# The first decode batch's keys move into the last half pair of the prompt attention, and the attention's second group takes key blocks by two

## The chip, the cores and the metric

The kernel runs on one core of a Trainium2 chip. The metric is the device time of one execution in microseconds, from the start to the end of the program. Five engines run side by side, each through its own list of instructions in order: TensorE (matrix products and turns of blocks), VectorE, ScalarE, GpSimd, and SyncE, which issues transfers. They wait for each other on semaphores.

## What is computed

One inference step of a small hybrid decoder with two layers: a gated short convolution, then attention with forget gates over shared keys and values. It takes a prompt of 1024 tokens and, beside it, eight decode batches of eight tokens each, with 1024 past positions in pages of 128 that a table names. Cut to the two attentions:

```python
def prompt_attention(q, k, v, logf):          # 16 heads of 64, causal, by blocks of 128 queries
    s = einsum('bqhd,bkhd->bhqk', qb, k) * scale + c[t] - c[s]
    p = softmax(where(kpos <= qpos, s, NEG_INF))
    return einsum('bhqk,bkhd->bqhd', p, v)

def sample_attention(q, k_new, v_new, logf_new, k_past, v_past, logf_past):
    s_past = einsum('bqhd,bkhd->bhqk', q, k_past) * scale + cn_q + rest
    s_new  = einsum('bqhd,bkhd->bhqk', q, k_new) * scale + cn_q - cn
    p = softmax(concatenate([s_past, where(causal, s_new, NEG_INF)]))
    return einsum(p_past, v_past) + einsum(p_new, v_new)

x = x + (o * silu(z)) @ w_out                 # then a gated input embedding and a norm
```

## The kernel before

All orders are written by hand, for each engine, with semaphores between them. Products of the layers are made in three passes of split operands (a high and a low part: `w_hi`, `w_lo`, `Hhi`, `Hlo`).

**Prompt attention.** Heads go in eight pairs, `j` = 0 to 7; a pair is two half pairs, one for each head. `STEPS` is the order of a half pair. `("S", qb)` makes the scores of query block `qb` (VectorE takes the row maximum, L1647, ScalarE the exponential, L1249, GpSimd the normalisation, L579). `("T", grp, kb)` turns the probabilities of key block `kb` for the four query blocks of a group (L891); ScalarE copies them to `pTh` (L1257), VectorE subtracts for `pTl` (L1658). `("V", grp, kb)` multiplies them with the values (L903). `("D", n)` puts in `n` of the 48 dense pieces that make the next pair's projections, three passes each (L844 to L846). Two PSUM banks and two buffers serve the turned blocks, by `kb % 2`. In the second group a piece stands before each value product, and the turn of block `kb + 2` after it.

The last pair has no next pair to project for: its first half has 24 pieces, ahead of its second group, its second half has none. The half pairs of the last pair are called (7,0) and (7,1) here.

**Decode batches.** After the prompt attention, `sample_batch(b)` follows the list `BATCH`. `("K", pg)` turns a page of keys in two halves of four blocks (`k_turn`, L952), into PSUM banks 5 and 6; ScalarE copies the first half to `KT` (L1359), VectorE the second (L1770). `("B",)` starts the scores with the bias rows `Bkeys` (L961) and adds the new keys' scores (L964), `("S", pp)` adds the scores of two pages (L973). `Y`, `T` and `V` are the softmax's turns and the values of the batch before, `("D", n)` the dense pieces of the output projection (`out_pieces`, L1021 to L1023), 16 for each batch. The first batch has no batch before it: it runs with `first=True`, keys and scores alone.

Before the output projection can start, the eight blocks of the prompt's y have to be split into `Hhi` (ScalarE, `y_hi`, L1362) and `Hlo` (VectorE, `y_lo`, L1774); seven of them come back from memory. Before the first batch VectorE clears and fills the fixed rows of `Bkeys` (L1847 to L1852, semaphore `s_ones`) and arranges the queries (`prepare`); GpSimd then loads the bias rows (`load_sample`, L611 to L613).

Of the kernel before, what the change touches and what calls it, by code (L numbers as in the profile page):

```python
# [24 lines left out]
P = 128  # L25
D = 1024
# [38 lines left out]
         ("S", 6), ("D", 6), ("V", 0, 1), ("T", 0, 3), ("S", 7), ("D", 6), ("V", 0, 2), ("D", 1), ("V", 0, 3), ("D", 5),  # L65
         ("T", 1, 0), ("T", 1, 1)]
for _kb in range(8):
    STEPS += [("D", 1 if _kb < 7 else 2), ("V", 1, _kb)] + ([("T", 1, _kb + 2)] if _kb < 6 else [])
# [12 lines left out]
         ("K", 6), ("V", 5), ("V", 6), ("K", 7), ("V", 7), ("D", 4), ("S", 3)]  # L81
LAST = [("D", 3), ("Y",), ("T", 0), ("T", 1), ("T", 2), ("D", 2), ("V", 0), ("V", 1), ("V", 2), ("V", 3), ("D", 4),
# [20 lines left out]
def program(nc, a, o, d):  # L103

    es = ExitStack()
    with es:
# [37 lines left out]

        sh = ExitStack()
# [80 lines left out]
        SS = flat[:, 2 * 512:2 * 512 + NK]  # L226
        dcn = nc.dram_tensor("new_key_sums", (DB, 2, H, DS), F32, kind="Internal").ap()
# [21 lines left out]
        names += [f"k_in{i}" for i in range(RING)] + [f"v_in{i}" for i in range(RING)]  # L249
# [44 lines left out]
        def _(sp):  # L294
# [121 lines left out]
            def half1(j, more):  # L416
# [53 lines left out]
            for pg in range(RING):  # L470
                load_keys(0, pg, first=True)
            sp.wait_ge(sems["pv"], START["pv"] + 24 * NPAIR)
            load_x(0, 0)
            sample_loads(0, 0, x=False, tile=False)
# [41 lines left out]
        def _(g):  # L516
# [68 lines left out]

            def iteration(j, more):
                for hh in range(2):
                    if more and hh == 0:
                        gain_b1(j, 0, 1)
# [17 lines left out]
            def load_sample(b):  # L607

                rows = bass.ds(H * b, H)
                for x in range(2):  # L610
                    g.dma_start(f(Bk[H * x:H * x + H, 0:KEYS]), d["rest"][rows, x, 0:KEYS]).then_inc(sems["s_bk"], 16)  # L611
                    g.dma_start(f(Bk[H * x:H * x + H, KEYS:]), d["rest"][rows, x, bass.ds(KEYS + DS * b, DS)]).then_inc(sems["s_bk"], 16)
                g.dma_start(f(Ar[R_CN:R_CN + 2, :]), dcn[bass.ds(b, 1)].rearrange("b x h t -> (b x) (h t)")).then_inc(sems["s_bk"], 16)  # L613

# [29 lines left out]
            g.wait_ge(sems["s_restout"], 48)  # L644
            g.wait_ge(sems["s_ones"], 1)
            g.wait_ge(sems["kv_out"], START["kv_out"] + 64 * NPAIR)
# [6 lines left out]
            g.wait_ge(sems["s_all"], 1)  # L653
            load_sample(1)
# [13 lines left out]
        def _(pe):  # L668
# [237 lines left out]

            def half_pair(j, half, more):
                p = 0
                for step in STEPS:
# [34 lines left out]
            def k_turn(b, pg):  # L944

                pe.wait_ge(sems[f"k_in{pg % RING}"], 16 * (PAGES // RING * b + pg // RING) + 16)
                for c in range(2):
                    pe.wait_ge(sems[f"s_kt{c}"], START[f"s_kt{c}"] + PAGES * b + pg)
                    if pg == 2 and not (isinstance(b, int) and b == 0):
# [61 lines left out]
            def out_pieces(m, par, q0, n):  # L1011

                for q in range(q0, q0 + n):
                    blk, k = divmod(q, KC)
                    if q == 0:
# [12 lines left out]
            def sample_batch(b, par, first=False):  # L1028

                q = 0  # L1030
                for step in BATCH:
# [6 lines left out]
                    if step[0] == "Y" and not first and not (isinstance(b, int) and b == 1):  # L1038
                        s_y_turn(b - 2)
                    if step[0] == "T" and not first:  # L1040
                        s_p_turn(b - 1, step[1], PAGES * b + 2)
                    if step[0] == "V" and not first:
                        s_values(b - 1, step[1])
                    if step[0] == "D" and not first:
                        q = out_pieces(b - 1, 1 - par, q, step[1])

            pe.wait_ge(sems["s_ones"], 1)
# [48 lines left out]
        def _(act):  # L1096
# [208 lines left out]
            def beside(j, half, p, attend, more):  # L1305
# [58 lines left out]
            def probabilities(b):  # L1364

                act.wait_ge(sems["s_max"], b + 1)
                af(Ps[:, :], SS, ACT.Exp, bias=small[:, 0:1], accum_out=small[:, 1:2])
# [10 lines left out]
            def sample_batch(b, par, i):  # L1378
# [3 lines left out]
                keep_keys(b, 1)  # L1382
                turned_probabilities(b - 1)
                keep_keys(b, 2)
                keep_keys(b, 3)
                w_hi((N_B2 + par) % 2, B_B2 + 2 * b - 2, loaded(N_B2 + par, 2, i))
                for pg in range(4, PAGES):
                    keep_keys(b, pg)

            act.wait_ge(sems["o_done"], START["o_done"] + 4 * NPAIR)  # L1390
            y_hi(NPAIR - 1, yT[:, 0:SEQ])
            w_hi(N_B2 % 2, B_B2 - 3, loaded(N_B2))
            for pg in range(PAGES):
                keep_keys(0, pg)
# [527 lines left out]
```

## Time and profile before

| what | us |
|---|---|
| median of three runs | 1876.99 (1875.25 to 1880.03) |
| the profiled execution | 1878.54 |
| its span, first to last instruction | 1876.8 |
| TensorE busy in it | 1729.0 (92%) |
| VectorE, ScalarE, GpSimd busy | 861.3, 672.8, 324.1 |

The span is what the trace covers; the profiled execution's time holds a little more around it. Busy time of TensorE counts matrix products whose ends are modelled. The granted clock is told as a share of TensorE's full speed, so 1.00 is 2.4 GHz and 0.50 is 1.2 GHz. A time in brackets behind an instruction is the idle time of its engine before it, with what ended it.

### The profile page before, as it was taken

The page shows a single profiled execution, that of the slowest core. Times are in us where ns is not written, and L with a number is a line of the kernel's source. Part 1 is how long each engine was busy: PE and PEld are TensorE (multiplying, and loading weights), DVE is VectorE, ACT ScalarE, POOL GpSimd, SP SyncE. Part 2 cuts the span into 40 slices and gives each one's busy share as a digit, 9 for nine tenths or more (in the row PEclk, how much of TensorE's full clock was granted, in tenths as well). Part 3 has the DMA queues.
Part 4 walks back from the last instruction along what each step waited for, and adds up shares of the span by engine and source line. Part 5 has one row for each costly group of instructions (what it writes and reads, how often), then busy time and mean ns, then how long its engine had stood idle before and what let it go on. Part 6 is the DMA issues. An engine that isn't in the chain of part 4 may idle for free.

```text
span 1876.8 us, 31182 instructions
## 1 busy us (share of the span) xinstructions
PE 1729.0 (92%) x10970; PEld 1570.6 (84%) x10970; DVE 861.3 (46%) x1344; ACT 672.8 (36%) x1095; POOL 324.1 (17%) x343
## 2 busy tenths in 40 slices
PE   6999999999999958999999999999966999998997
PEld 5999999999989948988888888888844667668997
DVE  4433333334243375565555555555545333323343
ACT  5111111112043233565556565565543222213222
POOL 4111111100000021213222221213111222210110
PEclk8999999999999979999999999999967999996998
DMA  4111111111211023111111010212035797983102
GB/s 144 40 43 46 46 46 46 46 45 42 66 42 43 12 97 95 47 39 54 46 35 58 24 57 24 68 35 58 24 113 197 268 328 292 342 270 81 34 28 95
DMA packets 173147, 165.08 MB, mean 88 GB/s; under 512 B 19756, under 2 KB 149948, under 8 KB 172966
## 3 DMA queue, kind: packets, MB, share of 16 engines
q1 hardware_dynamic: 162342, 129.51, 22.0%
q0 software_dynamic: 10752, 34.89, 5.1%
q8 instruction: 30, 0.49, 0.1%
q14 instruction: 23, 0.19, 0.0%
HBM read 141.08 MB, written 23.29 MB: 88 GB/s over the span
## 4 chain that ended last, share of the span: by engine, by line
PE 74%; DVE 8%; issue 5%; ACT 4%; DMA 3%; DVEq 2%; ACTq 1%; POOL 1%; POOLq 0%; SPq 0%
PE PS L680 13%; PE PS L682 13%; PE PS L681 12%; PE PS L844 5%; PE PS L845 4%; PE PS L846 4%; PE PS L903 3%; PE PS L952 3%; PE PS L891 2%; DMA Vpages<-in_cache_v 2%; PE PS L874 2%; DVE small L1647 2%; DVE pTl L1658 2%; PE PS L973 1%; PE PS L1073 1%
## 5 line engine op out<-in xcount | busy, mean ns | idle before, releaser
L680 PE MATMUL PS<-Hhi,w_hi 128*128 128x364 f32 (+1 forms) x1344 | 446.2, 332 | 33.6 <-DVE Hlo L1481 28.5
L682 PE MATMUL PS<-Hhi,w_lo 128*128 128x364 f32 (+1 forms) x1344 | 444.7, 331 | 0.0
L681 PE MATMUL PS<-Hlo,w_hi 128*128 128x364 f32 (+1 forms) x1344 | 444.5, 331 | 0.0
L680 PEld LDWEIGHTS PS<-Hhi,w_hi 128*128 128x128 f32 x1344 | 256.1, 191 | 37.4 <-issue 23.9
L844 PE MATMUL PS<-Hhi,w_hi 128*128 128x364 f32 (+1 forms) x768 | 274.5, 357 | 0.1
L681 PEld LDWEIGHTS PS<-Hlo,w_hi 128*128 128x128 f32 x1344 | 256.2, 191 | 0.0
L682 PEld LDWEIGHTS PS<-Hhi,w_lo 128*128 128x128 f32 x1344 | 255.9, 190 | 0.0
L846 PE MATMUL PS<-Hhi,w_lo 128*128 128x364 f32 (+1 forms) x768 | 252.4, 329 | 0.0
L845 PE MATMUL PS<-Hlo,w_hi 128*128 128x364 f32 (+1 forms) x768 | 252.3, 329 | 0.0
L547 POOL TENSOR_TENSOR w_raw<-w_raw,GT 128x1024 f32<-128x1024 f32 x65 | 126.2, 1941 | 696.6 <-DMA w_raw<-in_w_kv 385.2
L1108 ACT ACTIVATE w_hi<-w_raw 128x1024 fp32r<-128x1024 f32 (+1 forms) x97 | 105.5, 1089 | 309.4 <-PE PS L682 294.2
L1431 DVE TENSOR_TENSOR w_lo<-w_raw,w_hi 128x1024 fp32r<-128x1024 f32 (+1 forms) x97 | 125.9, 1298 | 85.6 <-ACT w_hi L1108 83.6
L579 POOL TENSOR_SCALAR Pb<-Pb,small 128x128 f32<-128x128 f32 (+7 forms) x128 | 97.2, 763 | 376.3 <-DVE small L1652 376.3
L1658 DVE TENSOR_TENSOR pTl<-PS,pTh 128x512 fp32r<-128x512 f32 x192 | 103.5, 554 | 123.9 <-ACT pTh L1257 121.5
L1249 ACT ACTIVATE Pb<-PS,small 128x128 f32<-128x128 f32 (+7 forms) x128 | 94.8, 740 | 161.3 <-DVE small L1647 161.3
L844 PEld LDWEIGHTS PS<-Hhi,w_hi 128*128 128x128 f32 x768 | 147.0, 191 | 0.9 <-DVE w_lo L1431 0.4
L845 PEld LDWEIGHTS PS<-Hlo,w_hi 128*128 128x128 f32 x768 | 146.1, 190 | 0.0
L846 PEld LDWEIGHTS PS<-Hhi,w_lo 128*128 128x128 f32 x768 | 144.8, 189 | 0.0
L1257 ACT ACTIVATE pTh<-PS 128x512 fp32r<-128x512 f32 x192 | 89.9, 488 | 97.1 <-PE PS L891 93.4
L1647 DVE TENSOR_REDUCE small<-PS 128x1 f32<-128x128 f32 (+7 forms) x128 | 95.7, 748 | 39.1 <-PE PS L877 38.3
L903 PE MATMUL PS<-pTh,VS 128*128 128x512 f32 x192 | 73.9, 385 | 34.1 <-DVE pTl L1658 34.0
L891 PE MATMUL PS<-ident,Pb 128*128 128x128 f32 x576 | 95.1, 286 | 6.7 <-POOL Pb L579 6.7
(273 smaller groups left out, 2457.9 us busy)
## 6 DMA issues: line engine op xcount, KB each, us to landing
Kpages<-in_cache_k SPq DMA_DIRECT2D x64, 512.0 KB, 5.3
Vpages<-in_cache_v POOLq DMA_DIRECT2D x60, 512.0 KB, 6.3
w_raw<-in_w_in_a SPq DMA_DIRECT2D x64, 256.0 KB, 3.0
w_raw<-in_w_ple_gate SPq DMA_DIRECT2D x16, 512.0 KB, 3.6
w_raw<-in_w_kv SPq DMA_DIRECT2D x32, 256.0 KB, 3.1
w_raw<-in_w_in_b SPq DMA_DIRECT2D x32, 256.0 KB, 3.1
parked_x<-X SPq DMA_DIRECT2D x8, 544.0 KB, 5.2
X<-parked_x SPq DMA_DIRECT2D x8, 544.0 KB, 8.4
```

What stands on the lines that cost most here:

```text
L547: g.tensor_tensor(w, w, GT[:, :, r:r + 1].to_broadcast([P, KC, P]), ALU.mult).then_inc(sems["w_gained"], 1)
L680: mm(out, wh, hi[:, k, s:e], start=(k == 0), stop=False)
L681: mm(out, wh, lo[:, k, s:e], start=False, stop=False)
L682: last = mm(out, wl, hi[:, k, s:e], start=False, stop=(k == nk - 1))
L844: mm(out, wh, Hhi[:, k, s:e], start=(k == 0), stop=False)
L845: mm(out, wh, Hlo[:, k, s:e], start=False, stop=False)
L846: last = mm(out, wl, Hhi[:, k, s:e], start=False, stop=(k == KC - 1))
L891: last = tp(PS[:, 5 + kb % 2, qi * P:(qi + 1) * P], Pb[:, off:off + P], ident[:, :])
L903: last = mm(PS[:, 7, q0 * P:512], VS[:, kb, hh, :], x[:, kb % 2, q0 * P:512], start=(kb == 0 and x is pTh), stop=(kb == nkb - 1 and x is pTl))
L1431: tt_(wlo[:, par, 0:nk, :], raw[:, par, 0:nk, :], f(whi[:, par, 0:nk, :]), ALU.subtract).then_inc(sems["w_split"], 1)
L1647: ve.reduce_max(small[:, qb:qb + 1], score_bank(qb)[:, 0:n], AXX, negate=True).then_inc(sems["rowmax"], 1)
L1658: tt_(pTl[:, kb % 2, q0 * P:512], PS[:, 5 + kb % 2, q0 * P:512], f(pTh[:, kb % 2, q0 * P:512]), ALU.subtract).then_inc(sems["p_lo"], 1)
```

## The change

Three things are changed.

- `STEPS` takes the second group's key blocks in couples, in every half pair: two turns, some dense pieces, two value products, the next two turns. One dense piece moves from between the first group's last two value products to the second group.
- The first batch's page turns, scores and bias are put at numbered pieces of (7,1), where no dense piece stands (`FIRST`). They use a keys buffer of their own in the place of `Hhi` (`Kpages_first`, `KT_first`), PSUM bank 2 for both halves of a page and banks 0 and 1 for the scores. SyncE loads six pages once the last dense piece is done and two more as pages are turned; VectorE fills the fixed rows at piece 0 of (7,1); GpSimd loads the first batch's bias ahead of the second half's normalisations. The first batch of its own after the attention is gone.
- The second batch follows a list of its own, `SECOND`: its keys and scores and the first batch's softmax and values, and then all 16 output pieces. The eight splits of y, which stood beside the first batch, stand beside its page copies.

```diff
-         ("S", 6), ("D", 6), ("V", 0, 1), ("T", 0, 3), ("S", 7), ("D", 6), ("V", 0, 2), ("D", 1), ("V", 0, 3), ("D", 5),
-         ("T", 1, 0), ("T", 1, 1)]
-for _kb in range(8):
-    STEPS += [("D", 1 if _kb < 7 else 2), ("V", 1, _kb)] + ([("T", 1, _kb + 2)] if _kb < 6 else [])
+         ("S", 6), ("D", 6), ("V", 0, 1), ("T", 0, 3), ("S", 7), ("D", 6), ("V", 0, 2), ("V", 0, 3), ("D", 5),
+         ("T", 1, 0), ("T", 1, 1), ("D", 3), ("V", 1, 0), ("V", 1, 1), ("T", 1, 2), ("T", 1, 3),
+         ("D", 3), ("V", 1, 2), ("V", 1, 3), ("T", 1, 4), ("T", 1, 5), ("D", 2), ("V", 1, 4), ("V", 1, 5), ("T", 1, 6), ("T", 1, 7),
+         ("D", 2), ("V", 1, 6), ("V", 1, 7)]
...
+SECOND = [("K", 0), ("Y",), ("K", 1), ("T", 0), ("T", 1), ("B",), ("T", 2), ("S", 0), ("K", 2), ("V", 0), ("K", 3), ("V", 1), ("S", 1),
+          ("K", 4), ("V", 2), ("K", 5), ("V", 3), ("S", 2), ("V", 4), ("V", PAGES),
+          ("K", 6), ("V", 5), ("K", 7), ("V", 6), ("S", 3), ("V", 7), ("D", 16)]
+FIRST = {2: [("B",)], 44: [("N",)]}
+for _u in range(4 * PAGES // 2):
+    FIRST[3 + 10 * (_u // 4) + 2 * (_u % 4)] = [("K", _u // 2, _u % 2)]
+for _pp in range(4):
+    FIRST[12 + 10 * _pp] = [("S", _pp)]
...
                 if not more:
                     sp.wait_ge(sems["block_done"], START["block_done"] + B_B2)
+                    for pg in range(RING + 2):
+                        sp.dma_start(Kf[:, pg, :], ck[page(0, pg), :]).then_inc(sems[f"k_first{pg}"], 16)
                     sp.wait_ge(sems["y_out"], START["y_out"] + 16 * (NPAIR - 1))
                     for k in range(NPAIR - 1):
                         sp.dma_start(f(Hlo[:, k, 0:SEQ]), d["y"][k]).then_inc(sems["y_back"], 16)
+                    for pg in range(RING + 2, PAGES):
+                        rows = page(0, pg)
+                        sp.wait_ge(sems["s_kturn"], 2 * (pg - RING - 2) + 2)
+                        sp.dma_start(Kf[:, pg - RING - 2, :], ck[rows, :]).then_inc(sems[f"k_first{pg}"], 16)
...
             def iteration(j, more):
                 for hh in range(2):
+                    if hh == 1 and not more:
+                        g.wait_ge(sems["s_restout"], 48)
+                        g.wait_ge(sems["s_ones"], 1)
+                        g.wait_ge(sems["kv_out"], START["kv_out"] + 64 * NPAIR)
+                        load_sample(0)
...
-            load_sample(0)
             g.wait_ge(sems["pv"], START["pv"] + 24 * NPAIR)
             for pg in range(RING):
                 load_values(0, pg)
+            g.wait_ge(sems["s_all"], 1)
+            load_sample(1)
...
+            def f_turn(pg, c):
+                if c == 0:
+                    pe.wait_ge(sems[f"k_first{pg}"], 16)
+                    pe.wait_ge(sems["s_kt1"], START["s_kt1"] + pg)
+                else:
+                    pe.wait_ge(sems["s_kt0"], START["s_kt0"] + pg + 1)
+                for i in range(4 * c, 4 * c + 4):
+                    last = tp(PS[:, 2, (i % 4) * P:(i % 4 + 1) * P], Kf[:, pg % (RING + 2), i * P:(i + 1) * P], ident[:, :])
+                last.then_inc(sems["s_kturn"], 1)
+            def f_bias():
+                pe.wait_ge(sems["act_evac"], EA_B2)
+                pe.wait_ge(sems["s_prep"], 1)
+                pe.wait_ge(sems["s_bk"], 80)
+                for c0 in (0, 512):
+                    mm(SF[:, c0:c0 + 512], Ar, Bk[:, c0:c0 + 512], start=True, stop=False)
...
                             if more or PIECES * half + p < 24:
                                 dense_piece(j, half, p)
+                            elif half == 1:
+                                first_batch(p)
...
-            sample_batch(0, 0, first=True)
-            pe.wait_ge(sems["h_ready"], 40)
-            sample_batch(1, 1)
+            sample_batch(1, 1, SECOND)
...
+                if half == 1 and not more:
+                    for step in FIRST.get(p, ()):
+                        if step[0] == "K" and step[2] == 0:
+                            act.wait_ge(sems["s_kturn"], 2 * step[1] + 1)
+                            act.wait_ge(sems["s_score"], START["s_score"] + step[1] // 2)
+                            af(KTf[:, 0:4, step[1] % 2 * P:(step[1] % 2 + 1) * P], PS[:, 2, :].rearrange("p (i n) -> p i n", i=4),
+                               ACT.Copy).then_inc(sems["s_kt0"], 1)
...
+                if half == 1 and not more:
+                    if p == 0:
+                        first_batch_rows()
+                    for step in FIRST.get(p, ()):
+                        if step[0] == "K" and step[2] == 1:
+                            ve.wait_ge(sems["s_kturn"], 2 * step[1] + 2)
+                            ve.wait_ge(sems["s_score"], START["s_score"] + step[1] // 2)
+                            ve.tensor_copy(KTf[:, 4:8, step[1] % 2 * P:(step[1] % 2 + 1) * P],
+                                           PS[:, 2, :].rearrange("p (i n) -> p i n", i=4)).then_inc(sems["s_kt1"], 1)
...
+                if first:
+                    y_lo(1, f(Hlo[:, 1, 0:SEQ]), 35)
+                    y_lo(2, f(Hlo[:, 2, 0:SEQ]), 36)
```

## Rows read from the trace of the kernel before

**Rows 1.** Stages: length; busy PE, PEld, DVE, ACT, POOL; PEclk, DMA share, GB/s.

```profile
1371.40:1379.20 7.80, 7.09 (x26) 5.72 (x26) 3.39 (x5) 2.39 (x4) 0.00 (x1) 0.50 0.87 274
...
1383.30:1420.40 37.10, 26.38 (x94) 19.00 (x93) 16.06 (x32) 13.17 (x30) 5.96 (x8) 0.59 0.17 57
1420.40:1452.80 32.40, 19.11 (x148) 12.51 (x148) 20.72 (x29) 13.77 (x18) 7.81 (x15) 0.76 0.65 222
1452.80:1484.70 31.90, 30.67 (x281) 21.25 (x277) 11.12 (x20) 7.70 (x13) 7.29 (x14) 0.98 0.77 275
```

**Rows 2.** TensorE's waits, 753 to 1370 us: total, times, longest.

```profile
PE PS L903 <- DVE pTl L1658: 31.0, 34, 1.8
```

**Rows 3.** Timeline of TensorE, second group of (6,0): start, length, instruction.

```profile
1288.74 1.03 PE L891 MATMUL PS<-ident,Pb 128*128 128x128 f32 x8
...
1291.49 0.50 PE L903 MATMUL PS<-pTh,VS 128*128 128x512 f32 x1 [1.23 <-DVE pTl L1658]
...
1292.42 0.41 PE L844 MATMUL PS<-Hhi,w_hi 128*128 128x360 f32 x1
...
1293.00 0.39 PE L903 MATMUL PS<-pTh,VS 128*128 128x512 f32 x1
...
1293.46 0.60 PE L891 MATMUL PS<-ident,Pb 128*128 128x128 f32 x4
...
1300.87 0.28 PE L874 MATMUL PS<-KA,QA 128*128 128x128 f32 x1
```

**Rows 4.** The same of (6,1): the first value product, and the next pair's first score.

```profile
1332.92 0.50 PE L903 MATMUL PS<-pTh,VS 128*128 128x512 f32 x1 [1.78 <-DVE pTl L1658]
...
1344.20 0.30 PE L874 MATMUL PS<-KA,QA 128*128 128x128 f32 x1
```

**Rows 5.** Timeline of ScalarE and VectorE: one turned block's copy and subtraction.

```profile
1292.70 0.60 ACT L1257 ACTIVATE pTh<-PS 128x512 fp32r<-128x512 f32 x1 [1.87 <-PE PS L891]
...
1293.33 0.69 DVE L1658 TENSOR_TENSOR pTl<-PS,pTh 128x512 fp32r<-128x512 f32 x1 [1.30 <-ACT pTh L1257]
```

**Rows 6.** Timeline of TensorE in the last pair, (7,0)'s second group and (7,1).

```profile
1371.46 1.97 PE L891 MATMUL PS<-ident,Pb 128*128 128x128 f32 x8 [3.51 <-POOL Pb L579]
...
1383.29 0.28 PE L874 MATMUL PS<-KA,QA 128*128 128x128 f32 x1
...
1390.18 0.79 PE L874 MATMUL PS<-KA,QA 128*128 128x512 f32 x1 [1.59 <-ACT Pb L1249]
...
1391.64 1.70 PE L891 MATMUL PS<-ident,Pb 128*128 128x128 f32 x7
1393.69 0.79 PE L874 MATMUL PS<-KA,QA 128*128 128x512 f32 x1 [0.34 <-ACT Pb L1249]
```

**Rows 7.** Timeline of VectorE, GpSimd and TensorE: the way to the first bias.

```profile
1385.53 0.61 DVE L1647 TENSOR_REDUCE small<-PS 128x1 f32<-128x128 f32 x2
...
1422.88 0.92 DVE L1847 MEMSET Bkeys<- 32x1032 f32 x1 [0.33 <-issue]
...
1427.17 0.71 POOL L611 DMA_DIRECT2D Bkeys<-key_bias  x1 [19.11 <-DVEq L1852]
...
1432.40 0.71 PE L961 MATMUL PS<-Bkeys,w_hi 72*128 72x512 f32 x3 [1.54 <-issue]
```

**Rows 8.** Timeline of TensorE in the first batch: page turns and scores.

```profile
1434.42 3.44 PE L952 MATMUL PS<-ident,Kpages 128*128 128x128 f32 x16
1439.12 1.07 PE L973 MATMUL PS<-KT,w_raw 128*32 128x256 f32 x16 [1.26 <-DVE KT L1770]
1440.12 1.09 PE L952 MATMUL PS<-ident,Kpages 128*128 128x128 f32 x8
...
1444.36 1.93 PE L973 MATMUL PS<-KT,w_raw 128*32 128x256 f32 x16 [1.71 <-DVE KT L1770]
```

**Rows 9.** Timeline of ScalarE and VectorE: one block of y split.

```profile
1428.38 1.05 ACT L1362 ACTIVATE Hhi<-Hlo 128x1024 fp32r<-128x1024 f32 x1
...
1429.88 1.21 DVE L1774 TENSOR_TENSOR Hlo<-Hlo,Hhi 128x1024 fp32r<-128x1024 f32 x1
```

More of the change, by code:

```diff
@@ L470, in _ @@
             for pg in range(RING):
-                load_keys(0, pg, first=True)
+                load_keys(1, pg, first=True)
             sp.wait_ge(sems["pv"], START["pv"] + 24 * NPAIR)
             load_x(0, 0)
-            sample_loads(0, 0, x=False, tile=False)
             sample_loads(1, 1)
@@ L606, in _ @@
             iteration(NPAIR - 1, False)
[L607 to L613, printed above, removed]
             def load_new(b):
@@ L905, in pv_step, with f_scores, f_new, first_batch @@
                 last.then_inc(sems["pv"], 1)
+            def f_turn(pg, c):
[13 more added lines that the diff above has]
+                    mm(SF[:, c0:c0 + 512], Ar, Bk[:, c0:c0 + 512], start=True, stop=False)
+            def f_scores(pp):
+                pe.wait_ge(sems["s_kt0"], START["s_kt0"] + 2 * pp + 2)
+                pe.wait_ge(sems["s_kt1"], START["s_kt1"] + 2 * pp + 2)
+                for e in range(2):
+                    for g_ in range(4):
+                        last = mm(SF[32 * g_:32 * g_ + 32, 256 * pp:256 * pp + 256], qc[:, 0, g_, e, :], KTf[:, 2 * g_ + e, :],
+                                  start=False, stop=(pp % 2 == 1 and e == 1))
+                last.then_inc(sems["s_score"], 1)
+            def f_new():
+                pe.wait_ge(sems["s_kt1"], START["s_kt1"] + PAGES)
+                mm(SF[:, KEYS:], Ar, Bk[:, KEYS:], start=True, stop=False)
+                for e in range(2):
+                    for g_ in range(4):
+                        last = mm(PS[32 * g_:32 * g_ + 32, 2, 0:DS], qc[:, 0, g_, e, :], knb[:, 0, 2 * g_ + e, :], start=False, stop=(e == 1))
+                last.then_inc(sems["s_all"], 1)
+            def first_batch(p):
+                for step in FIRST.get(p, ()):
+                    if step[0] == "B":
+                        f_bias()
+                    if step[0] == "K":
+                        f_turn(step[1], step[2])
+                    if step[0] == "S":
+                        f_scores(step[1])
+                    if step[0] == "N":
+                        f_new()
             def half_pair(j, half, more):
@@ L1026, in out_pieces, with sample_batch @@
                 return q0 + n
-            def sample_batch(b, par, first=False):
+            def sample_batch(b, par, steps=BATCH):
                 q = 0
-                for step in BATCH:
+                for step in steps:
                     if step[0] == "K":
@@ L1366, in probabilities @@
                 act.wait_ge(sems["s_max"], b + 1)
-                af(Ps[:, :], SS, ACT.Exp, bias=small[:, 0:1], accum_out=small[:, 1:2])
+                af(Ps[:, :], SF if isinstance(b, int) and b == 0 else SS, ACT.Exp, bias=small[:, 0:1], accum_out=small[:, 1:2])
                 act.drain().then_inc(sems["s_exp"], 1)
@@ L1388, in sample_batch @@
                     keep_keys(b, pg)
[L1390 to L1394, printed above, removed]
-                if pg == 0:
-                    act.wait_ge(sems["y_back"], 16 * (NPAIR - 1))
-                if pg < NPAIR - 1:
-                    y_hi(pg, f(Hlo[:, pg, 0:SEQ]))
-            sample_batch(1, 1, 0)
+                    if first and pg < 7:
+                        for k in (2 * pg - 7, 2 * pg - 6):
+                            y_hi(k, f(Hlo[:, k, 0:SEQ]))
+            sample_batch(1, 1, 0, first=True)
             with act.Fori(0, 3) as i:
@@ L1796, in largest @@
                 ve.wait_ge(sems["s_score"], START["s_score"] + 4 * b + 4)
-                ve.reduce_max(small[:, 0:1], SS, AXX, negate=True).then_inc(sems["s_max"], 1)
+                ve.reduce_max(small[:, 0:1], SF if isinstance(b, int) and b == 0 else SS, AXX, negate=True).then_inc(sems["s_max"], 1)
             def probabilities(b):
@@ L1822, in out_block, with sample_batch @@
                 add_x(m, PS[:, blk, :], 512 * blk, 512 * blk + 512).then_inc(sems["dve_evac"], 1)
-            def sample_batch(b, par, i, more=True):
+            def sample_batch(b, par, i, more=True, first=False):
                 mi = i if par else i - 1
@@ L1831, in sample_batch @@
                 keep_keys(b, 1)
+                if first:
+                    y_lo(NPAIR - 1, yT[:, 0:SEQ], 33)
                 probabilities(b - 1)
@@ L1834, in sample_batch @@
                 keep_keys(b, 3)
-                out_block(b - 1, 1 - par, mi, 0)
+                if first:
+                    w_lo(N_B2 % 2, N_B2)
+                    y_lo(0, f(Hlo[:, 0, 0:SEQ]), 34)
+                else:
+                    out_block(b - 1, 1 - par, mi, 0)
                 keep_keys(b, 4)
+                if first:
+                    y_lo(1, f(Hlo[:, 1, 0:SEQ]), 35)
+                    y_lo(2, f(Hlo[:, 2, 0:SEQ]), 36)
                 w_lo((N_B2 + par) % 2, N_B2 + b)
-                keep_keys(b, 5)
-                keep_keys(b, 6)
+                for pg in (5, 6):
+                    keep_keys(b, pg)
+                    if first:
+                        for k in (2 * pg - 7, 2 * pg - 6):
+                            y_lo(k, f(Hlo[:, k, 0:SEQ]), 34 + k)
                 if more:
```

87 lines of the change are left out of this document (51 added, 36 removed).

## The prediction

> **What bounds the kernel now.** Read the stages first [rows 1]: how long each is, how much of it TensorE works, and at which of its two levels (1.2 and 2.4 GHz). The last half pair of the prompt attention (1383.3 to 1420.4, 37.1 us) has no dense products to fill it: TensorE is busy 26.4 us of it, at a granted clock of 0.59, so mostly at the lower level. The first batch's keys (1420.4 to 1452.8, 32.4 us) fill it no better: 19.1 us, clock 0.76. The second batch (31.9 us) has dense products between its steps: busy 30.7 us, clock 0.98. So the change works on 101.4 us in which TensorE idles or is slow, and on 14 filled half pairs.
>
> Then the waits of TensorE in the prompt attention [rows 2]: 34 waits for `pTl`, 31.0 us in all, about 2.2 us a half pair. The timeline says where: in a half 0 one wait of 1.23 us before the second group's first value product [rows 3]; in a half 1 one of 1.78 us there and more behind it, the group lasting until 1344.20 [rows 4].
>
> **Key blocks by two, in 14 filled half pairs.** No work is added: 10 pieces instead of 9 stand in the group, one moved down from the group before it. From [rows 3] a piece after a turn takes 0.58 us (1292.42 to 1293.00) and 0.5 after another, a value product 0.46, a turn of four blocks 0.35. A block turned is ready for its product about 1.7 us after its turn: 0.28 hand-over, 0.6 copy on ScalarE, 0.69 subtraction on VectorE, small hand-overs [rows 5]; the second block of a couple follows about 0.6 later. Three pieces behind the first two turns are 1.58 us where one was 0.58, so the first wait shrinks by about 0.7 to 0.9 us. It doesn't vanish, since the first subtraction stands behind VectorE's output of the group before, which I leave where it is. Behind blocks 2 and 3 a turn and three pieces (1.9 us) cover the 1.7. Behind blocks 4 and 5 there are two pieces only (0.25 + 1.08): a new wait of about 0.4 us. Behind 6 and 7, half 1: ScalarE's evacuation of the last dense tile now stands ahead of the copies of blocks 6 and 7, and waits for VectorE's `q_lo`; a new wait of 1.2 us. Laid out, half 0 ends at 1300.26 where [rows 3] has 1300.87 (gain 0.6 us), half 1 at 1342.95 where [rows 4] has 1344.20 (1.25 us): 1.86 us x 7 pairs = **-13.0 us**. Bounds: -31 (all waits of [rows 2] gone) and -3 (each new couple waits about 1 us: 28 us in place of 31).
>
> **The half pair before the last, (7,0)**, has no pieces there, so a couple can't be covered: two turns, 1.7 us until ready, two products. At the lower level, which it had from 1371.4 to 1379.2 [rows 1], two turns are 1.4 us and two products 2.0: T10 at 1371.46, products at 1374.07, 1375.1, then 1378.6, 1379.6, 1382.95, 1384, 1386.3, 1386.8, end 1387.2 against 1383.29 [rows 6]. At full clock it ends where it did. I take **+3.5 us** (0 to +4).
>
> **The last half pair, (7,1).** Added to TensorE: bias rows (two passes), 16 half turns of pages (0.86 us at the lower level, 0.55 at the higher [rows 8]), four score steps (1.93 or 1.07 us), the new keys. TensorE has idle time for them, but all engines run their lists in order, so where each stands counts. Times from its first score (1383.29) on.
>
> The bias stands at piece 2, ahead of the second score. It needs rows that VectorE clears only once it has come to piece 0, behind the first row maximum, which it starts at 1385.53 [rows 7] (+2.2; done by +2.6). From the first clearing (1422.88) to GpSimd's first load is 4.3 us, from that load (1427.17) to the bias 5.2 us [rows 7]. So the bias starts at 2.6 + 4.3 + 5.2 = **+12.1**, and TensorE waits nearly all of that; before, the second score followed at once. GpSimd's eight normalisations queue behind these loads, but the first turn needs them much later.
>
> From there each half turn uses one bank: the turn, a copy (0.6 or 0.69 as in [rows 5]), 0.15 of hand-over, the next turn. ScalarE's copy stands behind its exponential, so from the fifth score on the page's second half turn, the block turns behind it and the next score all wait for the exponential and then run one after the other; before, the block turns (1.70 us) stood inside that wait and score followed score after 3.51 us [rows 6]. Stage by stage, at the lower level until about +39 and in a few stretches at the higher (before: after): to the second score 0.3 : 13.1; to the fifth 6.6 : 7.9; to the sixth 3.5 : 7.6; to the seventh 3.9 : 6.6; to the eighth 4.3 : 6.3; to the group's turns 6.3 : 12.9 (here page 5's second half, scores 2, two products, both halves of page 6 and the first of page 7 follow each other behind the eighth exponential); to the end 12.3 : 12.9. Sum 37.1 : 67.3, **+30 us**. All at the higher level it is 12.6, 6.4, 4.6, 5.3, 5.0, 10.8, 10.9 = 55.6 (+18.5), all at the lower 74 (+37).
>
> One rule bears on which level. In this trace page turns ran at the lower level for 3.44 us from 1434.42, and the next scores, at 1439.12, at the higher (1.07 us) [rows 8]: the clock rose over a stretch that held only turns. The Trainium skill says in "TensorE: Matmul & The Clock Gate", Part 4: PE-mode transpose, that the full clock does not engage for transposes, which do not count as busy in the same way. By that rule turned pages would not help the last half pair's clock, and the sum would be that of the lower level, given among the rivals; the trace does not agree as far as these rows go.
>
> SP's queue: six first pages are loaded ahead of the seven blocks of y, some 20 us before TensorE asks for them; the last two pages wait for the first turns, and the output weights queue behind them, wanted only in the tail. Hidden by the last pair; if the pages came late, TensorE would wait at the first turn.
>
> **The tail.** Removed: the first batch's own 32.4 us. In place of 32.4 + 31.9 = 64.3 us [rows 1] one batch runs without dense products between its steps, with all eight conversions of y (1.05 us each on ScalarE, 1.21 on VectorE [rows 9]) and the products at its end. From the half pair's end: output and first pages as before; the bias of the second batch at about 12.0, since GpSimd issues four value pages ahead of its loads (as late as the first batch's before, 1432.40 - 1420.4 [rows 7], with other work ahead of it); from there VectorE sets the pace, six page copies 0.69, seven subtractions 1.21, two weight splits 1.22, preparation 0.6 = 15.7 us, with some 6.5 us of waiting for ScalarE and TensorE between them: 34.2; last scores and values 1.6: 35.8; 16 pieces, 48 passes at 0.23 (half of a value product, [rows 3]): 46.9; and 0.8 because the next row maximum now follows the last output block: 47.7. At the lower clock steps grow, and the first pieces too: 55.5. Middle **51.5, so -12.8 us** (-16.6 to -8.8). Cover given up: before, 16 dense pieces filled the second batch; now they stand alone, 11 us.
>
> **Sum:** -13.0 + 3.5 + 30.0 - 12.8 = **+7.7 us**. The profiled execution took 1878.54 us (span 1876.8); the runs' median is 1876.99, 1.5 us lower. 1878.5 + 7.7 - 1.5 = **1884.7 us**.
>
> **Rivals.** A: TensorE has the higher level through the last pair and the tail. For it: more work between its waits, and 0.98 in the filled batch; against it: from 1390.18 a score, seven turns and the next score followed each other with one pause of 0.34 us, and all ran at the lower level (1.70 us for seven turns [rows 6]). Sum -13.0 + 0 + 18.5 - 16.6 = -11.1, 1865.9 us, faster; it counts as faster once the last half pair lasts under some 59 us. B: the lower level throughout: -13.0 + 4 + 37 - 8.8 = +19.2, 1896 us. The Trainium skill's rule on transposes ("TensorE: Matmul & The Clock Gate", Part 4) would bring this one about. C: by-two ordering removes all 31 us of waits: 7.7 - 18 = -10.3, 1867 us; against it, VectorE's late first subtraction. D: it only moves them (saves 3): +17.7, 1895 us; the 1.2 us wait behind `q_lo` speaks for it.
>
> **Chances.** A measurement tells about 0.3%, 5.6 us, from no change. My sum (-3 to +14, 1874 to 1891): 0.47, of it slower 0.31, same 0.14, faster 0.02. A 0.18 (faster 0.16, same 0.02), B 0.20 (slower), C 0.08 (faster 0.06, same 0.02), D 0.07 (slower 0.06, same 0.01). Together slower 0.57, same 0.19, faster 0.24. The range takes in A to D: 1865 to 1897.
>
> **What would show it.** Right: TensorE waits about 11 us before the bias in the last half pair, which lasts 60 to 72 us; page copies on ScalarE behind each exponential; the first dense output piece some 36 to 42 us after that half pair's end and batch 2's keys 47 to 55 after it; waits for `pTl` near 18 us. Wrong: no wait at the bias, score following score as quickly as before, or half pairs that keep 2.2 us of waits each.

## The result, and the profile after

The changed kernel takes 1887.26 us (median of 5 runs, 1885.98 to 1888.56), the kernel before 1878.04 us beside it (5 runs): a ratio of 1.0054 [1.0043, 1.0066], slower by some 10 us. The forecast was 1884.7 us, slower. The profiled execution has a span of 1885.7 us, 8.9 us above that of before.

Where the 8.9 us come from, by the places that the prediction named. Each length runs from one mark of TensorE to the next, in either trace; the row of the seven pairs runs from the attention's first score to the second group's first turns of (7,0), so it holds (7,0)'s first group too.

| stretch | before | after | difference | forecast |
|---|---|---|---|---|
| up to the attention's first score | 752.92 | 753.98 | +1.1 | 0 |
| seven filled pairs | 618.54 | 609.79 | -8.8 | -13.0 |
| rest of (7,0) | 11.83 | 13.11 | +1.3 | +3.5 |
| (7,1) | 37.1 | 62.9 | +25.8 | +30.0 |
| from there to batch 2's keys | 64.3 | 54.1 | -10.2 | -12.8 |
| batch 2's keys to the end | 392.1 | 391.8 | -0.3 | 0 |

The stages around the prompt's end, after, by stretches of time (length; busy time and instructions of TensorE, its weight loads, VectorE, ScalarE and GpSimd; granted clock; share and rate of the transfers). The rows answer to [rows 1]: the end of (7,0), then (7,1), then the second batch with all output pieces.

```profile
1363.70:1376.90 13.20, 9.90 (x43) 7.28 (x43) 5.17 (x9) 3.92 (x8) 0.01 (x1) 0.75 0.98 383
1376.90:1439.80 62.90, 39.40 (x241) 28.36 (x239) 24.71 (x50) 17.56 (x38) 8.64 (x13) 0.73 0.22 69
1439.80:1494.00 54.20, 38.80 (x279) 25.78 (x279) 22.23 (x30) 16.58 (x23) 12.45 (x24) 0.78 0.69 242
```

In (7,1) TensorE works 39.4 us of 62.9, so 23.5 us of it are waits. TensorE's waits after, from 1360 to 1495 us (line that waited, what it waited for, total, times, longest), name them:

```profile
PE PS L943 <- DMA w_hi<-new_key_sums: 10.6, 1, 10.6
PE PS L934 <- ACT KT_first L1404: 8.6, 6, 2.8
PE PS L1032 <- issue: 7.9, 1, 7.9
```

L943 is the first batch's bias (`f_bias`), L934 a half page's turn (`f_turn`), L1032 the second batch's bias (L961 before). The two waits ahead of biases are 18.5 us together. The timeline of TensorE in (7,1), after, at the scores (L893) that begin each step, and at the first turn of its second group:

```profile
1376.88 0.27 PE L893 MATMUL PS<-KA,QA 128*128 128x128 f32 x1
...
1387.95 1.19 PE L943 MATMUL PS<-Bkeys,w_hi 72*128 72x512 f32 x2 [10.61 <-DMA w_hi<-new_key_sums]
1388.94 0.42 PE L893 MATMUL PS<-KA,QA 128*128 128x256 f32 x1
...
1396.96 0.79 PE L893 MATMUL PS<-KA,QA 128*128 128x512 f32 x1 [0.74 <-ACT Pb L1320]
...
1403.22 0.48 PE L893 MATMUL PS<-KA,QA 128*128 128x512 f32 x1
...
1407.45 0.78 PE L934 MATMUL PS<-ident,Kpages_first 128*128 128x128 f32 x4 [2.77 <-ACT KT_first L1404]
...
1409.16 0.77 PE L893 MATMUL PS<-KA,QA 128*128 128x512 f32 x1
...
1414.81 0.48 PE L893 MATMUL PS<-KA,QA 128*128 128x512 f32 x1
...
1427.26 1.91 PE L910 MATMUL PS<-ident,Pb 128*128 128x128 f32 x8
```

What the bias waits for stands in the timeline of VectorE and GpSimd, after: the first row maximum, the first clearing of rows, GpSimd's first and last load.

```profile
1379.12 0.28 DVE L1729 TENSOR_REDUCE small<-PS 128x1 f32<-128x128 f32 x1
1379.67 0.92 DVE L1792 MEMSET Bkeys<- 32x1032 f32 x1 [0.27 <-issue]
...
1383.87 0.72 POOL L608 DMA_DIRECT2D Bkeys<-key_bias  x1 [20.15 <-issue]
...
1386.02 0.52 POOL L610 DMA_DIRECT2D w_hi<-new_key_sums  x1
```

And the half page that waits 2.77 us at 1407.45 stands behind this copy, which ScalarE makes only behind its exponential:

```profile
1405.92 0.90 ACT L1320 ACTIVATE Pb<-PS,small 128x768 f32<-128x768 f32 x1 [1.77 <-DVE small L1729]
...
1406.81 0.59 ACT L1404 ACTIVATE KT_first<-PS 128x512 f32<-128x512 f32 x1
```

The second batch, after: GpSimd's first and last value page, the bias loads behind them, and on TensorE the bias, the scores (L1044) with the longest wait for a page copy, the first output piece and batch 2's first page.

```profile
1441.42 0.62 POOL L602 DMA_DIRECT2D Vpages<-in_cache_v  x1 [19.54 <-issue]
...
1444.95 0.53 POOL L602 DMA_DIRECT2D Vpages<-in_cache_v  x1 [0.62 <-issue]
1445.47 0.50 POOL L608 DMA_DIRECT2D Bkeys<-key_bias  x1
...
1447.39 0.51 POOL L610 DMA_DIRECT2D w_hi<-new_key_sums  x1
...
1455.19 1.20 PE L1032 MATMUL PS<-Bkeys,w_hi 72*128 72x512 f32 x3 [7.90 <-issue]
...
1471.90 1.21 PE L1044 MATMUL PS<-KT,w_raw 128*32 128x256 f32 x16 [3.32 <-DVE KT L1881]
...
1482.75 0.51 PE L1095 MATMUL PS<-Hhi,w_hi 128*128 128x512 f32 x1
...
1493.86 1.03 PE L1023 MATMUL PS<-ident,Kpages 128*128 128x128 f32 x8
```

The bias stands 15.4 us behind the end of (7,1), and 7.3 us behind the end of its last issue, where the first batch's bias before followed its last issue in 2.6 us (1429.85 to 1432.40).

### The profile page after: what moved, and what is told of

Same layout as the page of the kernel before. It is cut to its first block and busy times, and to the rows that moved or that the text cites. A ratio compares the mean times of both kernels' runs of the same rounds, so it can differ in the third digit from the quotient of the medians.

```text
span 1885.7 us, 31178 instructions
## 1 busy us (share of the span) xinstructions
PE 1732.5 (92%) x10970; PEld 1568.3 (83%) x10970; DVE 857.9 (45%) x1344; ACT 669.1 (35%) x1095; POOL 326.1 (17%) x343
## 5 line engine op out<-in xcount | busy, mean ns | idle before, releaser
L1740 DVE TENSOR_TENSOR pTl<-PS,pTh 128x512 fp32r<-128x512 f32 x192 | 99.6, 552 | 122.5 <-ACT pTh L1328 122.3
L1328 ACT ACTIVATE pTh<-PS 128x512 fp32r<-128x512 f32 x192 | 85.6, 488 | 85.2 <-PE PS L910 82.1
L910 PE MATMUL PS<-ident,Pb 128*128 128x128 f32 x576 | 84.8, 280 | 6.1 <-POOL Pb L597 5.6
```

Source lines behind the costliest of these rows:

```text
L1740: tt_(pTl[:, kb % 2, q0 * P:512], PS[:, 5 + kb % 2, q0 * P:512], f(pTh[:, kb % 2, q0 * P:512]), ALU.subtract).then_inc(sems["p_lo"], 1)
```

## The experiments

My theory: the added turns, copies and scores are not what costs; it is where each stands in its engine's list. The rivals: the work itself fills the stretch (so that a wait taken away comes back one step later), or the clock level decides. In the last run a third question is put: whether the move is worth anything at all. Differences in us are the ratios' differences times 1877.

**The couples alone, and the move alone.** The first kernel is the kernel before with the new `STEPS`; the second is the changed kernel with the old order in the filled pairs.

```diff
 (in the second kernel)
-                for step in STEPS:
+                for step in (FILLED_STEPS if more else STEPS):
```

> The kernel before with the new STEPS and nothing else. My sum, with the terms now read from the trace of after (filled half pairs -8.4, half pair (7,0) +1.3): about 7 us faster than before, 1871 us, and (7,1), which has no pieces, about 1 us longer, so 6 us. Rival (couples only move the waits): within 3 us of before. Rival (the gain seen in the trace of after comes from something else in it, such as the earlier start of transfers): no gain here at all.

Measured: 1870.86 us (before 1877.45), ratio 0.9965 [0.9954, 0.9976], 6.6 us faster.

> After, with the old STEPS in pairs 0 to 6, so that the first batch's move stands alone. If the move costs what the trace of after shows (last half pair +25.8, (7,0) +1.3, tail -10.3), this is 17 us slower than before, about 1895 us, and about 8 us slower than after. Rival (the move is near neutral and the couples cost): as before or faster, and faster than after.

Measured: 1899.24 us, ratio 1.0118 [1.0104, 1.0133], 22 us slower, where 17 were expected. So one part of the change gains and the other loses; the loss of the move is three times the couples' gain. The two don't add up (22 - 7 = 15, where the change has 10): the profiled span is 10.8 us longer than the changed kernel's, 8.0 in the seven pairs, 0.8 ahead of the attention and 3.0 behind batch 2's first keys, less 1.0 in between. Behind that mark the two kernels do the same work, so the 3.0 us stay open. In all the traces this last part takes 389.7 to 395.4 us, so a few us between two kernels need not come from their edits.

**The bias late.** The first batch's bias is put at piece 12, just ahead of its first scores; the first page's turn, now ahead of it, waits for the last dense tile as the bias does.

```diff
-FIRST = {2: [("B",)], 44: [("N",)]}
+FIRST = {44: [("N",)]}
...
-    FIRST[12 + 10 * _pp] = [("S", _pp)]
+    FIRST[12 + 10 * _pp] = ([("B",)] if _pp == 0 else []) + [("S", _pp)]
```

> After, with the bias made at piece 12, just ahead of the first scores that add to it, instead of piece 2. If the wait of 10.6 us at the bias lengthens the last half pair: the second score follows the first at once, pages 0 and 1 are turned in that time, 2 to 3 us of wait stay at the bias, and the kernel is about 8 us faster than after, 1879 us. Rival (page turns and copies are what bind, and merely wait elsewhere): less than 3 us faster.

Measured: 1881.59 us, ratio 1.0026 [1.0015, 1.0037], 5 us less than the changed kernel, where 8 were expected. The bias wait of 10.6 us is gone, but 7.7 us of it stand at page 0 now. The timeline of this kernel's three engines shows why:

```profile
1384.10 0.42 DVE L1731 TENSOR_REDUCE small<-PS 128x1 f32<-128x256 f32 x1
...
1384.56 0.47 ACT L1322 ACTIVATE Pb<-PS,small 128x256 f32<-128x256 f32 x1 [4.88 <-DVE small L1731]
...
1385.66 1.11 PE L936 MATMUL PS<-ident,Kpages_first 128*128 128x128 f32 x4 [7.73 <-ACT KT_first L1406]
```

VectorE clears the rows from 1379.45 to 1384.0; the second row maximum stands behind that, the second exponential behind the maximum, ScalarE's copy of page 0 behind the exponential, and the page's second half behind the copy. The clearing held two things, and only one of them had been moved.

**The bias loads first.** GpSimd loads the second batch's bias ahead of the four value pages.

```diff
             g.wait_ge(sems["s_table"], 16)
+            g.wait_ge(sems["s_all"], 1)
+            load_sample(1)
             g.wait_ge(sems["pv"], START["pv"] + 24 * NPAIR)
             for pg in range(RING):
                 load_values(0, pg)
-            g.wait_ge(sems["s_all"], 1)
-            load_sample(1)
```

> After, with GpSimd's loads of the second batch's bias rows ahead of the four value pages instead of behind them. If their place in the queue makes the wait of 7.9 us at the second bias: that wait goes, VectorE's conversions of y bind instead, and the kernel is 5 to 7 us faster than after, about 1881 us. Rival (the page and y transfers crowd the engines, or y's conversions bind anyway): within 2 us of after.

Measured: 1877.07 us, ratio 1.0001 [0.9992, 1.001], 10 us less than the changed kernel, more than expected: the whole loss. By the traces some 9 us of it stand between (7,1)'s end and batch 2's keys. The order of five short loads undoes what the change as a whole cost. The transfers (issue, size, median us from issue to landing), first of the changed kernel, from 1441 to 1449 us:

```profile
Bkeys<-key_bias POOLq DMA_DIRECT2D x2, 64.0 KB, 7.7
Bkeys<-key_bias POOLq DMA_DIRECT2D x2, 0.5 KB, 7.5
```

and of this one, from 1430 to 1440 us:

```profile
Bkeys<-key_bias POOLq DMA_DIRECT2D x2, 64.0 KB, 2.3
Bkeys<-key_bias POOLq DMA_DIRECT2D x2, 0.5 KB, 1.9
```

In the changed kernel 4.05 us of issues stand ahead of the loads (1441.42 to 1445.47), and each takes some 5.4 us more to land, with 2 MB of value pages ahead of it.

**Pages across the scores.** The bias late, and each page's two halves on the two sides of a block of scores. The second kernel has this, the old order in (7,0) and the bias loads first.

```diff
+FIRST = {p: [("K", u // 2, u % 2)] for u, p in enumerate((5, 6, 8, 9, 15, 16, 20, 21, 26, 27, 32, 33, 35, 38, 40, 41))}
+FIRST.update({12: [("B",), ("S", 0)], 22: [("S", 1)], 34: [("S", 2)], 42: [("S", 3)], 44: [("N",)]})
```

> As the run with the bias late (1881.6 us), but each page's two half turns stand on the two sides of a block of scores, so that the copy of the first half is taken by ScalarE in the gap before the exponential that the second half would have waited for. If the place of the steps in the engines' lists is the cost, a page no longer makes TensorE wait behind an exponential from the fifth score on (8.6 us in 6 waits in the changed kernel), and of the 7.7 us at page 0 some 3 go: 4 to 7 us less, 1875 to 1878 us, the last half pair near 50 us. If the added work itself (turns, copies, clock level) fills that half pair, nothing changes: 1880 to 1883 us.

Measured: 1881.22 us (before 1876.23), ratio 1.0022 [1.0011, 1.0032]. My expectation missed: it is within 1 us of the kernel with the bias late. TensorE's waits in this kernel, from 1372 to 1426 us:

```profile
PE PS L933 <- DVE KT_first L1834: 6.2, 4, 1.9
PE PS L950 <- DVE KT_first L1834: 5.6, 3, 2.3
PE PS L933 <- ACT KT_first L1403: 5.1, 2, 4.8
```

Fewer waits for ScalarE's copies (15.6 us with the bias late), and 11.8 us for VectorE's, which stand behind the row maxima. Here the rival was right, by its time: the wait changed its name. TensorE still waits, so it is not work that fills the half pair, but the copies behind the other engines' steps.

> The run above, the old order in the half pair before the last (1.3 us measured against it), and the second batch's bias loads ahead of the value pages (10.2 us measured alone). If these are separate waits, they add up: 1864 to 1867 us, below both kernels. If the tail is bound by VectorE's list whatever the loads do, and the earlier end only lengthens its waits, under half of it: 1870 us or more.

Measured: 1869.71 us, ratio 0.9961 [0.9948, 0.9974]; 11.4 us less than the kernel with the split pages, where the two parts had 1.3 (read from the trace, not run by itself) and 10. So they are separate waits and add up; the forecast missed by what the split pages did not bring.

**The rows cleared early.** VectorE clears the rows in (7,0), where it stood idle for 4.0 us; the bias stays at piece 2. The second kernel adds this to the one above, the third takes the late bias and the split pages out of it again.

```diff
-                    if p == 0:
-                        first_batch_rows()
...
+                if half == 0 and not more and p == 24:
+                    first_batch_rows()
```

> The changed kernel, but VectorE clears the bias rows in the half pair before the last (in the 4.0 us in which it stood idle ahead of 1359.3), so that the loads follow the normalisations of that half pair; the bias stays at piece 2. If the bias wait is a matter of the chain clearing, loads, bias, the 10.6 us wait ahead of the bias goes, and the steps behind it move up: 8 to 10 us less than the changed kernel, 1877 to 1879 us. If the last half pair is bound by the page copies and exponentials behind the bias, most of the wait comes back there: 1883 us or more.

Measured: 1878.23 us, ratio 1.0008 [0.9999, 1.0018], 8.6 us less than the changed kernel, as the theory said: cleared early, neither the bias nor the second maximum waits.

> The run with all moves, with the rows cleared early too: the second row maximum and exponential are no longer held up behind the clearing, so page 0 waits no 7.7 us. If waits are the cost, 3 to 6 us less than that run: 1859 to 1863 us. If the half pair is bound by work by then, the same as it within 1.5 us.

Measured: 1864.74 us, ratio 0.9926 [0.9914, 0.9939], 6.6 us less than without the early clearing, a little more than the 3 to 6 expected.

> The run with all moves and the rows cleared early, without the late bias and without the pages across the scores: bias at piece 2 and page halves where the changed kernel has them. If the two waits ahead of the biases and the half pair before the last are all there is, their parts add up (8.6 + 10.2 + 1.3 us against the changed kernel, which gives 20 us): 1866 us, at most 2 us more than the run with everything. If the place of the page halves matters by itself, 3 to 6 us more than that run: 1868 to 1871 us.

Measured: 1863.81 us (before 1877.84), ratio 0.9926 [0.9913, 0.994], the same as with the late bias and the split pages. So the late bias and the page halves' place are worth nothing that these runs can tell (within some 3 us), and two edits of a few lines, with the old order in (7,0), turn 10 us of loss into 14 us of gain. What remains in this kernel, from 1360 to 1495 us, is chiefly copies: ScalarE's in (7,1), which stand behind its exponentials, and VectorE's in the second batch, which stand behind the conversions of y and a weight split.

```profile
PE PS L940 <- ACT KT_first L1410: 10.3, 6, 2.8
PE PS L1050 <- DVE KT L1887: 6.3, 3, 3.3
```

The clock has a part in this gain. Over (7,1) and the stretch behind it TensorE is busy 78.2 us of 117.1 in the changed kernel, at granted clocks of 0.73 and 0.78, and 68.4 us of 93.1 in this one, at 0.90 and 0.88 (columns as in [rows 1]):

```profile
1374.94:1423.89 48.95, 33.44 (x241) 23.92 (x240) 20.81 (x40) 17.11 (x38) 8.45 (x13) 0.90 0.31 106
1423.89:1468.01 44.12, 34.96 (x277) 23.45 (x278) 22.23 (x30) 16.34 (x23) 10.01 (x19) 0.88 0.83 294
```

So of the 24 us between the two kernels here some 14 are waits, and some 10 the same work done in less time at the higher clock. The edits touch orders alone; that the clock rose because the waits went is argued and not shown by a run of its own.

**The gate product later.** This tests the filled pairs, which gained 8.8 us and not 13. The timeline of the changed kernel at the start of a half 0's second group (VectorE, GpSimd and TensorE), the first score of the half 1 behind it, and that half's product with the gate:

```profile
1281.85 1.91 POOL L565 TENSOR_TENSOR w_raw<-w_raw,GT 128x1024 f32<-128x1024 f32 x1
...
1282.18 2.12 DVE L1749 TENSOR_TENSOR yT<-yT,zf 64x512 f32<-64x512 f32 x1
1284.24 1.27 DVE L1740 TENSOR_TENSOR pTl<-PS,pTh 128x512 fp32r<-128x512 f32 x2
...
1284.96 0.50 PE L922 MATMUL PS<-pTh,VS 128*128 128x512 f32 x1 [0.45 <-DVE pTl L1740]
...
1294.18 0.27 PE L893 MATMUL PS<-KA,QA 128*128 128x128 f32 x1
...
1323.54 0.69 DVE L1749 TENSOR_TENSOR yT<-yT,zf 64x512 f32<-64x512 f32 x1
```

The first group's output times its gate (L1749) stands ahead of the first subtractions, and takes 2.12 us beside GpSimd's product, 0.69 elsewhere. The product was put behind the first two subtractions, in the kernel with the rows cleared early and all moves, and in the kernel with the couples alone.

```diff
...
                         p_lo(j, half, step[1], step[2])
+                        if step[1:] == (1, 1):
+                            gated(half, 0)
```

> The run with all moves and the rows cleared early, and in every half pair VectorE multiplies the first group's output with its gate behind the first two subtractions of the second group, where it stood ahead of them (0.69 us in a half 1; 2.13 us in a half 0, where it overlaps a product of GpSimd). If the wait of the second group's first value products (0.45 us in a half 0, 0.77 us in a half 1) is what this product costs, about 0.45 and 0.7 us go, seven times: 6 to 8 us less, 1856 to 1859 us. If the subtractions are held up by GpSimd's product as the multiplication was, or the wait turns up behind the next couple, 0 to 3 us less: 1862 to 1865 us.

Measured: 1856.61 us, ratio 0.9887 [0.9872, 0.9902], 7.3 us less than with the product where it was.

> The kernel before with the key blocks by two alone (1870.9 us, 6.6 us below the kernel before), and the multiplication with the gate moved as in the run above. If that multiplication holds the first subtraction, the couples come to what was forecast for them: 6 to 8 us less, 1863 to 1865 us, near the 13 us below the kernel before. If not, 0 to 3 us less: 1868 to 1871 us.

Measured: 1862.73 us (1857.84 to 1862.95), ratio 0.9914 [0.99, 0.9927], 9.6 us less than the couples alone, more than the 6 to 8 expected, and 16 below the kernel before. Its five runs lie at two places, two at 1857.84 and 1857.87 and three from 1862.73 to 1862.95; the trace is of one of the first. A filled pair takes 81.8 us, where the couples alone give 83.2 and the kernel before 84.4. In its trace the subtractions are not held up by GpSimd's product (from 1273.87 here), and the first value product follows without a wait:

```profile
1275.28 1.29 DVE L1658 TENSOR_TENSOR pTl<-PS,pTh 128x512 fp32r<-128x512 f32 x2 [1.20 <-ACT pTh L1257]
1276.48 0.67 DVE L1673 TENSOR_TENSOR yT<-yT,zf 64x512 f32<-64x512 f32 x1
...
1276.38 0.40 PE L903 MATMUL PS<-pTh,VS 128*128 128x512 f32 x1
```

**The unmoved kernel, with the same mend.** The last kernel has the couples and the later gate product, and the first batch behind the attention as before; only its rows are cleared in (7,0) and its bias loaded at the start of (7,1).

> The run with the couples and the later gate product (1862.7 us), the first batch left behind the attention, but with its bias rows cleared and loaded early, as in the moved kernel: TensorE's 6.4 us wait ahead of the first page and the 1.5 us ahead of the bias have no cause then. If such waits are the gain to be had around the prompt's end and the move itself brings little, 6 to 8 us less, 0.983 to 0.988 of the kernel before: level with the moved kernel with all mends (0.9887). If the move, once mended, brings a gain of its own, this run stays at 0.990 to 0.992, because the page copies and y's conversions take the place of the wait.

Measured: 1855.82 us (before 1877.06), ratio 0.9886 [0.9869, 0.9902]: level with the moved kernel with all its mends (0.9887). The two edits bring it 5 us by the ratios, a little short of the 6 to 8; since the run without them lies at two places, it is 2 us beside its lower one and 7 beside its upper one. The traces show 3.6 us, between (7,1)'s first score and batch 2's first keys (99.0 and 95.4). The wait of 6.4 us ahead of the first page, which without the mend stands behind VectorE's clearing, is down to this, with 1.2 us more for ScalarE's copy behind it:

```profile
1407.77 1.28 PE L953 MATMUL PS<-ident,Kpages 128*128 128x128 f32 x8 [2.47 <-issue]
```

From (7,1)'s first score to batch 2's first keys this kernel takes 95.4 us and the moved one with all mends and the later gate product 96.7; the kernel before took 101.4, the changed one 117.0. So the first batch costs about as much inside (7,1) as behind it. The two kernels are not alike in all else: this one has the couples in (7,0), which cost it 1.4 us there (13.1 against 11.7), and the moved kernel with the bias at piece 2 (ratio 0.9926, 93.1 us in this stretch) was not tried with the later gate product. So a few us either way are left open.

## Why the prediction was right

The direction and the time were right (1884.7 forecast, 1887.26 measured). Each term of the sum had the right sign and came out smaller than forecast, gains and losses alike: the errors of +4.2, -2.2, -4.2 and +2.6 us cancelled. That the time came out within 3 us is in part luck.

- **Filled pairs, -13.0 forecast, -8.8 measured.** The step that was off is "the first wait shrinks by about 0.7 to 0.9 us" taken as a gain of 0.6 in a half 0 and 1.25 in a half 1: the periods fell by 0.16 and 1.0 us. In a half 0 the wait of [rows 3] did shrink, from 1.23 to 0.45 us, but chiefly because more pieces stand ahead of it. From the first value product to the end of the half pair it is 9.38 us before [rows 3] and 9.22 after (1284.96 to 1294.18, shown with the gate product), so that product stands almost as late in its half pair as it did. What held it was VectorE's product with the gate, part of the output that I left "where it is": with that put later a half 0 takes 0.84 us less and a half 1 0.58. In a half 1, with a piece fewer ahead of it, the first turn now reaches its normalisation too early and waits about 0.3 us for GpSimd (2.1 us over the seven pairs, none before). Of the two new waits that were forecast, the 0.4 us behind blocks 4 and 5 did not come; the 1.2 us behind 6 and 7 in a half 1 came as 0.85. The waits of TensorE after, from 754 to 1364 us, answer to [rows 2]: 16.2 us where 31.0 were and near 18 forecast, so neither C (none left) nor D (only moved) came about; of the second row, 3.5 us are (7,0)'s, which before had them too.

```profile
PE PS L922 <- DVE pTl L1740: 16.2, 22, 1.8
PE PS L910 <- POOL Pb L597: 5.6, 8, 3.5
```

- **(7,0), +3.5 forecast, +1.3 measured.** I took the lower level for its whole second group; the granted clock of the stretch was 0.75, so part of it ran at the higher. The old order there was not run by itself.
- **The first batch's bias, +12.1 forecast, +11.07 measured**, by the chain that was forecast: maximum, clearing, GpSimd's loads. The wait is 10.61 us, forecast about 11.
- **The rest of (7,1).** Stage by stage (first to second score, to the fifth, sixth, seventh, eighth, the turns, the end): forecast 13.1, 7.9, 7.6, 6.6, 6.3, 12.9, 12.9; measured 12.1, 8.0, 6.3, 5.9, 5.7, 12.4, 12.5. From the sixth score on the steps stand behind the exponentials as forecast, and are shorter. Both clock levels alternate in them, the higher one more than I took: the granted clock was 0.50 from 1388 to 1394 us, 0.89 from 1403.2 to 1409.2, 0.73 over the whole. Neither level throughout (A and B) came about. The rule on transposes that was named with B does not agree with the rows of the last section.
- **The tail, -12.8 forecast, -10.2 measured.** The step that failed is the bias of the second batch "at about 12.0": it stood at 15.4, since its loads land only behind the value pages (7.7 us after issue, 2.3 when issued first). The first output piece came at 43 (forecast 36 to 42), batch 2's keys at 54.1 (47 to 55).
- **What the prediction did not ask** is what the loss consists of. It priced the two bias waits as parts of the move. The runs show that they hang on the place of the clearing and of the loads, that 24 us lie between the kernel as changed and the one with three orders put right, and that with the later gate product added the moved and the unmoved kernel end level.

## What to carry to other kernels

When a piece of work is moved into a stretch with idle time, follow the inputs of its first step back through every engine's list: here the moved products were cheap, and the small clearing and loads ahead of them, standing where they did, made the whole loss. Before calling a move good or bad, give the unmoved kernel the same mends: here both end at 0.989 of the kernel before, so nothing could be measured that the move itself brought, in the forms that were run. And where two copies share one bank between two engines, putting the turns elsewhere only renames the wait, if each copy still stands behind that engine's exponential or maximum.

## What the runs showed of the hardware

VectorE's product of two tensors in SBUF takes 2.12 us while GpSimd's product (1.91 us) runs, and 0.69 us without it; it ends 0.54 us after GpSimd's does, as if it had started only about then. A subtraction with one operand in PSUM that began 0.50 us before the end of such a product was not held up (1.29 us for two, as in the other couples). The Trainium skill says this in "SBUF — State Buffer", section "SBUF: two separate sides": an instruction of VectorE with two SBUF inputs and one of GpSimd that reads SBUF exclude each other for a whole instruction; the trace agrees. Moving that one product was worth 7 to 10 us, as much as the change cost. Not all of it is this exclusion: by the traces of the two kernels with the couples, with the product early and late, some 6 us are gained in the seven half 0s, where GpSimd's product stood beside it, and 4 in the half 1s, where none did.

Short loads of 0.5 KB issued by GpSimd behind four pages of 512 KB landed 7.5 us after issue, and 1.9 us when issued ahead of them. In the first case transfers moved 360 GB/s in that stretch, in the second 64, so the place in the queue and the traffic are not told apart.

The granted clock rose while TensorE did nothing but turn blocks. After, its only work from 1442.32 to 1446 us was 16 turned blocks of pages, behind 2.52 us of idleness, and then eight more turned blocks:

```profile
1442.32 3.53 PE L1023 MATMUL PS<-ident,Kpages 128*128 128x128 f32 x16 [2.52 <-DVE yT L1749]
1446.05 1.24 PE L1055 MATMUL PS<-ident,Ps 128*128 128x128 f32 x8 [0.20 <-ACT KT L1437]
```

and by stretches (columns as above) the clock went from 0.50 to 0.95, ahead of the end of the first 16 at 1445.85, and was 1.00 behind that:

```profile
1444.30:1445.30 1.00, 1.00 (x5) 0.83 (x6) 0.69 (x1) 0.85 (x2) 0.38 (x2) 0.50 1.00 365
1445.30:1446.30 1.00, 0.80 (x7) 0.59 (x6) 0.41 (x1) 0.99 (x2) 1.00 (x3) 0.95 0.90 332
```

The rule of the Trainium skill in "TensorE: Matmul & The Clock Gate", Part 4: PE-mode transpose, that the full clock does not engage for transposes, does not agree with these rows. The turns are `pe.transpose` in the kernel, with the identity as one operand; that this is the mode which the page means is taken from its name, and the trace lists them as MATMUL.
